# Three middle chunks of two feed-forward layers: from written-out TensorE code to a hardware loop

## The reference

```python
def conv_ffn(h, buf, w_in, w_conv, b_conv, w_out):
    z, new_buf = causal_dwconv(h @ w_in, buf, w_conv, b_conv)
    return (jax.nn.gelu(z[..., :D_FF]) * z[..., D_FF:]) @ w_out, new_buf
```

## Time and profile before

| what | value |
|---|---|
| time, median of 3 runs | 3530.01 us (3529.58 to 3532.29) |
| the profiled execution's own time | 3529.58 us |
| its span, first to last instruction | 3527.8 us |
| mean granted TensorE clock | 0.942 of full speed |
| PE busy | 3164.6 us (90%) |
| DVE, POOL, ACT busy | 1709.7, 1107.3, 952.2 us |

### The profile page before, as it was taken

How to read it: one execution, slowest core, us unless ns; L and a number is a source line. 1 busy time by engine, 2 the same in 40 slices (tenths; PEclk the granted TensorE clock), 3 DMA queues, 4 the chain that set the end, 5 groups by cost and what they waited for, 6 DMA issues and landing times. The chain is left out here.

```text
span 3527.8 us, 55959 instructions
## 1 busy us (share of the span) xinstructions
PE 3164.6 (90%) x22204; PEld 2853.7 (81%) x22204; DVE 1709.7 (48%) x3168; ACT 952.2 (27%) x1486; POOL 1107.3 (31%) x803
## 2 busy tenths in 40 slices
PE   7997879999999986979777999799788999999996
PEld 5886869999999985969544666566678999999995
DVE  3675264444444347350358887700236454454445
ACT  4553141112011013021124777600123121111111
POOL 1322323333333331323003555400222333333331
PEclk8998999999999998989769999999799999999997
DMA  5223122122121121210244000066211111111112
GB/s 194 76 76 128 48 112 79 66 72 73 72 84 68 47 90 79 93 73 31 108 143 138 2 2 2 6 223 221 84 54 65 48 49 43 48 48 48 47 44 105
DMA packets 74998, 272.56 MB, mean 77 GB/s; under 512 B 8538, under 2 KB 19170, under 8 KB 72562
## 3 DMA queue, kind: packets, MB, share of 16 engines
q1 hardware_dynamic: 72786, 253.71, 20.4%
q10 hardware_dynamic: 1984, 15.62, 1.2%
HBM read 245.47 MB, written 33.10 MB: 79 GB/s over the span
## 5 line engine op out<-in xcount | busy, mean ns | idle before, releaser
L1491 POOL TENSOR_TENSOR w_hi<-w_raw,misc 128x1024 fp32r<-128x1024 f32 x197 | 376.5, 1911 | 1958.9 <-PE PA L1681 823.1
L1493 POOL TENSOR_TENSOR w_lo<-w_raw,w_hi 128x1024 fp32r<-128x1024 f32 x197 | 498.6, 2531 | 28.3 <-issue 0.4
L1681 PE MATMUL PA<-hB_hi,w_hi 128*128 128x344 f32 x1512 | 327.5, 325 | 58.2 <-DVE hB_lo L1857 34.7
L1681 PE MATMUL PB<-hB_hi,w_hi 128*128 128x344 f32 x1488 | 318.6, 323 | 17.7 <-DVE hB_lo L1857 17.7
L1681 PE MATMUL PB<-hB_lo,w_hi 128*128 128x344 f32 x1488 | 317.6, 322 | 18.5 <-POOL w_lo L1493 18.5
L1681 PE MATMUL PA<-hB_lo,w_hi 128*128 128x344 f32 x1512 | 323.6, 323 | 0.0
L1681 PEld LDWEIGHTS PA<-hB_hi,w_hi 128*128 128x128 f32 x1512 | 255.1, 190 | 65.1 <-issue 46.9
L420 DVE SCALAR_TENSOR_TENSOR zb<-ub,vec,zb 128x1024 f32<-128x1024 f32 x48 | 158.4, 3300 | 297.2 <-ACT zb L388 297.2
L1681 PE MATMUL PA<-hB_hi,w_lo 128*128 128x344 f32 x1416 | 301.1, 321 | 0.0
L1681 PE MATMUL PB<-hB_hi,w_lo 128*128 128x344 f32 x1392 | 294.1, 320 | 0.0
L1681 PEld LDWEIGHTS PB<-hB_lo,w_hi 128*128 128x128 f32 x1488 | 253.5, 190 | 18.8 <-POOL w_lo L1493 18.8
(11 more groups left out here) (444 smaller groups left out, 6155.7 us busy)
## 6 DMA issues: line engine op xcount, KB each, us to landing
w_raw<-in_w SPq DMA_DIRECT2D x197, 512.0 KB, 3.5
mt<-in_mw SPq DMA_DIRECT2D x48, 1024.0 KB, 5.0
pages<-in_pages SPq DMA_DIRECT2D x64, 384.0 KB, 4.2
x_dram<-X SPq DMA_DIRECT2D x3, 4128.0 KB, 11.2
X<-x_dram SPq DMA_DIRECT2D x3, 4128.0 KB, 12.4
mw<-in_mw SPq DMA_DIRECT2D x4, 2048.0 KB, 22.3
vall<-in_pages_v SPq DMA_DIRECT2D x64, 128.0 KB, 2.7
X<-in_xT SPq DMA_DIRECT2D x4, 1032.0 KB, 8.2
```

The lines of the kernel that those rows point to most:

```text
L1491: pool.tensor_tensor(w_hi[b], w_raw[b], zero.broadcast_to([P, 1024]), ALU.add)
L1493: pool.tensor_tensor(w_lo[b], w_raw[b], w_hi[b].bitcast(F32), ALU.subtract).then_inc(sem("w_split"), 1)
L1681: mm = pe.matmul(PS[ps][:, c, 0:CH], w[:, w0:w0 + P], x[:, k, c * CH:(c + 1) * CH], start=(k == 0 and n == 0), stop=(k == K - 1 and n == 2))
```

## The change

PE's Python loop over chunks 1 to 4 becomes a call of `rolled`: chunk 1 is written out, and chunks 2, 3 and 4 are one body that a hardware loop runs three times. This happens once for each layer, as `ffn_pe` is called for both. Chunks 0 and 5 stay written out. Every other engine's program stays as it is, and so do PE's matmuls and their order.

```diff
@@ -512,8 +512,7 @@
                 if mod:
                     ffn_mod(pe, c, p)
 
-        for c in range(1, CHUNKS - 1):
-            chunk(c, l == 0)
+        rolled(pe, 1, CHUNKS - 1, lambda c: chunk(c, l == 0))
         if l == 0:
             fold_of(pe, 32, PD[:, 6 * NC:8 * NC])
         chunk(CHUNKS - 1, False)
```

## The result

| kernel | median | range | runs |
|---|---|---|---|
| before | 3530.01 us | 3528.05 to 3532.29 | 5 |
| after | 3545.75 us | 3543.97 to 3551.56 | 5 |

The change makes the kernel slower by 0.6%: ratio 1.006, 95% interval 1.0046 to 1.0074, 15.7 us by the medians. Nine more executions of the changed kernel were timed, from 3546.09 to 3559.14 us; the median of all fourteen is 3551.7 us, which is 21.7 us above before, so 15.7 us may be too small. One of the nine is the profiled execution: it took 3550.26 us with a span of 3548.5 us, 20.7 us above the span of before.

The account below looks back on a forecast made before the run. PE, busy 3164.6 of 3527.8 us, was taken to bound the kernel. Profiled 3529.6 + 0.0 (fetching) + 0.0 (register waits) + 2 x 0.0 (layer 1) + 2 x 0.7 (layer 0) = 3531.0 us; range 3528 to 3546.

Parts of the forecast that it names:

- What bounds the kernel: Both feed-forward blocks: PE sets the end, so every delay put on it there lands on the kernel's end in full.
- Fetching saved: PE's instruction fetching for the removed chunk copies: it shows no pause now, so its disappearance saves 0.0 us.
- register counts: Waits in the loop body need register instructions, hidden by the sequencer's lead: 0.0 us; 25 us if that cover were gone.
- the branch itself: Branches back before chunks 3 and 4 in each layer: 0.21 us at the median, hidden by the sequencer's lead.
- That the branches back miss: All four branches back, two per layer: the long body's start is no longer held by PE and must be fetched.
- The price of a miss: At each branch back: 1.9 us for a small DMA's round trip plus 0.2 for the branch, 2.1 us.
- The rival of two round trips: Branches back: two dependent trips, 4.6 us a miss, exposing 1.6 us twice in layer 1, 3.2 twice in layer 0; chance 0.20.
- Only the first page matters: After a branch back only the target page is waited for; a page lasts 20 us, so the next comes meanwhile.
- The cover: Sequencer's lead at the branches: 3.0 us in layer 1, nothing exposed; 1.4 us in layer 0, 0.7 us exposed twice.
- The clock: After pauses on PE: 0.7 us costs no clock; pauses over 3 us drop to 1.2 GHz, 1.75 us each time.
- The forecast of no difference: Whole kernel: a difference under 0.2% (7.1 us), from a mostly hidden miss (0.57) or a kept body (0.15); chance 0.72.
- slower: Whole kernel: a long miss (0.20, 3542.7 us) or the sequencer falling behind (0.05, 3555 us); chance 0.25.

Follow-up runs that it names:

- hint: The changed kernel with a prefetch hint for the branch's target at the top of each loop iteration, in both layers: 3530.24 us, ratio 1.0005.
- small: The kernel before, with pairs 2 and 3 of chunks 1 to 4 of layer 1 as a two-iteration loop: 3528.07 us, ratio 0.9997.
- slot16: The changed kernel with the loop's first instruction placed at slot 16 of a 256-instruction block, in both layers: 3538.36 us, ratio 1.0032.
- slot239: The changed kernel with the loop's first instruction at slot 239 of a 256-instruction block, in both layers: 3553.32 us, ratio 1.0079.
- turned: As slot16, but each layer 0 iteration begins with the previous chunk's last modulation part, so the branch follows 72 long matmuls: 3532.83 us, one run.
- l1_only: The changed kernel with the loop in layer 1 alone, layer 0 written out as before: 3540.16 us, ratio 1.0032.
- hint239: As hint, with the loop's first instruction at slot 239 of a block, in both layers: 3530.99 us, ratio 1.0004.

## Why the prediction was wrong

**What bounds the kernel** was read rightly: every pause of PE came out at the end (17.9 us of pauses, 23.8 us in the two blocks with the clock, 20.7 us in the span, as the parts outside of the blocks were 3.1 us shorter in this execution).

**Fetching saved, register counts, the branch itself: 0.0 us each.** Right. `hint` has all three and stands at 1.0005, `small` at 0.9997.

**That the branches back miss.** Right for the changed kernel, and for the reason given. Not seen was that it hangs on where the body lies: the body of layer 1 is kept at slot 16 (7 blocks) and missed at slot 96 (8).

**The price of a miss, "one round trip of a small DMA", 2.1 us.** This is the step that failed. The branch lasts 3.5 to 4.1 us in the changed kernel and 3.3 us at the least where it misses in any other run. The block's own packet is 1.0 us as I had it; the rest is around it, and I had nothing but data transfers to price it by. The rival of two round trips, 4.6 us, was nearer, and its 3542.7 us is the nearest of my forecasts to the 3545.75 us measured; I gave it 0.20. That it comes so near is in part luck: it has pauses of 9.6 us where the trace has 17.9, because it knows nothing of the second pauses.

**"Only the first page matters."** The second failure, and the dearer one here: twice 4.75 us in layer 0. I had reasoned that a page lasts 20 us, so the next one can come meanwhile. It lasts 20 us from its first instruction; the branch enters it anywhere, and in layer 0 it entered with 7 instructions to go. `slot16` and `slot239` show the term by itself.

**The cover.** Right in kind and nearly in size: the branch of 3.90 us left a pause of 2.78 in layer 0, that of 3.84 left 1.50 in layer 1, so 1.1 and 2.3 us were covered where I had 1.4 and 3.0. `turned` shows it as a cause. The 3.0 us that I took for layer 1 was the lead of a wait; that of a branch, 2.6 us, stood in the earlier trace rows.

**The clock.** I had it for pauses over 3 us only. The 2.78 us pause brought the 1.2 GHz level already, and in `slot16` pauses of 2.23 and 2.16 us did (three loads 0.90 us), where layer 0 lost 9.3 us for 4.4 us of pauses. What the two blocks of the changed kernel lose beyond the pauses is 23.8 - 17.9 = 5.9 us, some 2 of it scatter. In the terms of the sum: 2 x (2.6 + 4.75) in layer 0 and 2 x 1.6 in layer 1 for the forecast's 2 x 0.7 and 0, and 4 to 6 for the clock. That is 22 to 24 us where I had 1.4, to be held against 20.7 us in the profiled span. The forecast of no difference (0.72) fell with that, and slower had 0.25. The range's upper end, 3546, just held the median of the five executions in the table, but not that of all fourteen, 3551.7 us.

## What to carry to other kernels

Before a loop replaces written-out code on the engine that sets the end, count the body's instructions and the blocks of 256 that it touches, its first slot included: up to 7 on PE went free here, 8 or 9 cost 3.3 to 4.1 us a branch back less what is queued ahead of it, and 1.5 to 4.8 us more when the first instruction lies near a block's end, besides what the lower clock takes. A prefetch hint for the branch took it away, but for pauses of 1.1 to 1.3 us in a loop of 9 blocks. And a long body's cost moves when unrelated code ahead of it changes (layer 1: 4.1 us in the changed kernel, 11.0 us in `l1_only`), so a single comparison of such a loop doesn't tell its price; the duration of the branch and the packets of the instruction queue do.

## What the runs showed of the hardware that was not expected

- A loop on PE is kept if it touches 7 blocks of its program without a hint (8 are missed), and 8 with one (layer 1 in `hint239`, 1760 instructions from slot 239; 9 are fetched anew). By that PE holds 8 blocks, 2048 instructions. The Trainium skill ("Runtime: NRT & Kernel Launch", section "Instruction fetch mechanics") gives 128 KiB for PE, and the runs agree with that. They do not agree with the window of two pages that it names in the same section: bodies of 777 and 1183 instructions, more than three and four blocks, were kept without a hint.
- The next block is not fetched together with a missed target: with 17 instructions or fewer to go PE paused a second time, for 3.3 to 4.8 us in layer 0 and 1.5 to 2.5 us in layer 1 (`slot239` and `l1_only`). Why layer 0 waits longer is not settled; the DMA engines are busy with data there (0.75 to 0.84 against 0.02).
- With the hint a body of up to 8 blocks isn't merely prefetched but stays: 139 packets in `hint` against 177 in the changed kernel.
- One such miss on a branch is three to four times the packet's own time (3.3 to 4.1 against 1.0 us).
